# The chunks of the split normalised x laid out with a step of 1040 bytes instead of 1024

## The reference

```python
def _swiglu(h, w_gu, w_down):
    gate, up = jnp.split(h @ w_gu, 2, axis=-1)
    return (jax.nn.silu(gate) * up) @ w_down

x = x + 0.5 * _swiglu(_rmsnorm(x, ffn1_norm), ffn1_w_gu, ffn1_w_down)
x = x + _token_mixing(_rmsnorm(x, mix_norm), w_in, ...)   # merged @ w_out inside
x = x + 0.5 * _swiglu(_rmsnorm(x, ffn2_norm), ffn2_w_gu, ffn2_w_down)
for l in range(2):
    shift, scale, gate = jnp.split(c_act @ w_ada[l] + b_ada[l], 3, axis=-1)
    h = _rmsnorm_2(x, norm_g[l]) * (1.0 + scale) + shift
    z = h @ w_in[l]                                       # 13 pieces of 512
    y = jnp.concatenate([o_fft, o_na, o_ret, o_cv], axis=-1) @ w_out[l]
    x = x + gate * y
```

## Time and profile before

| | |
|---|---|
| median of 3 runs | 3424.93 us (3423.47 to 3428.82) |
| the profiled execution, time | 3430.47 us |
| the profiled execution, span | 3428.7 us |
| mean granted TensorE clock | 0.972 of full speed |
| TensorE matmuls, busy | 3281.0 us (96% of the span) |
| weight loads, busy | 2880.8 us (84%) |
| VectorE, ScalarE, GpSimd, busy | 1777.6, 1456.5, 1780.0 us |
| memory read | 654.15 MB |

### The profile page before, as it was taken

How to read it: one execution, slowest core, us unless ns; L and a number is a source line. 1 busy time by engine, 2 the same in 40 slices (tenths; PEclk the granted TensorE clock), 3 DMA queues, 4 the chain that set the end, 5 groups by cost and what they waited for, 6 DMA issues and landing times.

```text
span 3428.7 us, 47162 instructions
## 1 busy us (share of the span) xinstructions
PE 3281.0 (96%) x19525; PEld 2880.8 (84%) x19525; DVE 1777.6 (52%) x2235; ACT 1456.5 (42%) x1893; POOL 1780.0 (52%) x738
## 2 busy tenths in 40 slices
PE   8999999998999999999999999998998998998988
PEld 6888888888998999887888888887988876998876
DVE  5554554422034478753555554433299654169763
ACT  5444443336554445444444444433333344343343
POOL 4444444437865765674444444444766544666543
PEclk9999999999998999999999999998999998999999
DMA  7887787865764554465888877764544344454444
GB/s 239 260 259 260 257 261 262 268 198 157 173 184 130 153 143 125 127 193 179 262 258 263 261 256 262 267 233 134 154 142 136 117 145 132 143 153 136 123 129 159
DMA packets 479357, 659.36 MB, mean 192 GB/s; under 512 B 63894, under 2 KB 267270, under 8 KB 478886
## 3 DMA queue, kind: packets, MB, share of 16 engines
q1 hardware_dynamic: 478462, 653.64, 60.7%
q0 software_dynamic: 352, 2.46, 0.2%
q10 hardware_dynamic: 328, 0.24, 0.0%
HBM read 654.15 MB, written 2.10 MB: 191 GB/s over the span
## 4 chain that ended last, share of the span: by engine, by line
PE 84%; DVE 11%; ACT 2%; issue 1%; POOL 1%; DMA 0%; ACTq 0%; DVEq 0%
PE ps L758 49%; PE ps L729 26%; DVE U L1834 4%; PE ps L719 2%; PE ps L937 2%; PE ps L954 1%; POOL split_slabs L694 1%; PE ps L1037 1%; DVE U L1718 1%; PE ps L907 1%; PE ps L783 1%; ACT split_slabs L1172 1%; DVE U L1660 0%; PE ps L1093 0%; PE ps L1133 0%
## 5 line engine op out<-in xcount | busy, mean ns | idle before, releaser
L694 POOL TENSOR_TENSOR split_slabs<-stage,split_slabs 128x1024 fp32r<-128x1024 f32 (+1 forms) x730 | 1777.2, 2439 | 1626.6 <-ACT split_slabs L1172 1624.7
L1172 ACT ACTIVATE split_slabs<-stage 128x1024 fp32r<-128x1024 f32 (+1 forms) x1032 | 1086.0, 1056 | 1758.5 <-PE ps L758 954.7
L758 PE MATMUL ps<-split_slabs,h_split 128*128 128x512 f32 x4992 | 1171.5, 396 | 23.2 <-DVE U L1953 12.9
L758 PEld LDWEIGHTS ps<-split_slabs,h_split 128*128 128x128 f32 x4992 | 941.2, 189 | 236.5 <-DVE U L1953 13.7
L729 PE MATMUL ps<-h_split,split_slabs 128*128 128x256 f32 x9072 | 1111.4, 284 | 9.9 <-DVE U L1887 8.0
L729 PEld LDWEIGHTS ps<-h_split,split_slabs 128*128 128x128 f32 x9072 | 1083.6, 193 | 34.3 <-issue 23.0
L1506 DVE TENSOR_TENSOR split_slabs<-stage,split_slabs 128x1024 fp32r<-128x1024 f32 x302 | 379.3, 1256 | 908.5 <-ACT split_slabs L1172 908.5
L758 PE MATMUL ps<-split_slabs,act_split 128*128 128x512 f32 x2112 | 482.1, 390 | 0.0
L758 PEld LDWEIGHTS ps<-split_slabs,act_split 128*128 128x128 f32 x2112 | 395.7, 188 | 82.1
L1834 DVE SCALAR_TENSOR_TENSOR U<-U,params 128x256 f32<-128x256 f32 x240 | 201.5, 910 | 0.0
L1522 DVE SCALAR_TENSOR_TENSOR U<-U,cact 128x512 f32<-128x512 f32 x192 | 189.1, 985 | 6.8
(11 more groups left out here) (196 smaller groups left out, 1650.6 us busy)
## 6 DMA issues: line engine op xcount, KB each, us to landing
stage<-in_w_in SPq DMA_DIRECT2D x360, 512.0 KB, 3.6
stage<-in_ffn_w_gu SPq DMA_DIRECT2D x352, 512.0 KB, 4.5
U<-in_w_ada SPq DMA_DIRECT2D x192, 512.0 KB, 5.8
stage<-in_ffn_w_down SPq DMA_DIRECT2D x176, 512.0 KB, 4.8
stage<-in_w_out SPq DMA_DIRECT2D x96, 512.0 KB, 3.9
stage<-in_w_in SPq DMA_DIRECT2D x80, 128.0 KB, 2.8
stage<-in_w_branch_c SPq DMA_DIRECT2D x32, 192.0 KB, 3.4
stage<-in_cmp_w SPq DMA_DIRECT2D x8, 512.0 KB, 3.8
```

What stands on the lines that cost most here:

```text
L694: nc.gpsimd.tensor_tensor(slab_part(n, 1, size(n)), stage[:, n % RING, 0:size(n)], slab_part(n, 0, size(n)).bitcast(F32), ALU.subtract).th ...
L758: ins = mm(ps[:, 2 * pair + T, :], stationary(kk, tp)[:, T * P:(T + 1) * P], w[wp][:, kk, :], start=first and kk == 0 and i == 0, stop=las ...
L1172: return fn(slab_part(n, 0, size(n)), stage[:, n % RING, 0:size(n)], ACT.Copy)
```

## The change

The step from one chunk of `h_split` to the next becomes 260 elements (1040 bytes) instead of 256 (1024 bytes). Every chunk still has 256 positions; the view `hx` cuts the four added elements off. The tensor grows by 2 x 16 x 16 = 512 bytes in each partition. To make room, `ssq`, `meansq` and `lnms` keep two places instead of six, used in turn (`r % 2`). By the declared sizes that gives 128 + 32 + 32 = 192 bytes back. So `stage` and what follows it up to `ssq` move by 512 bytes, and the arena by 320. Inside the arena nothing moves.

```diff
+HPAD = 4
...
-        hx = sbr("h_split", [P, 2, DC, S])
+        hx = sbr("h_split", [P, 2, DC, S + HPAD])[:, :, :, 0:S]
...
-        ssq = sb("ssq", [P, 6, TT, 4])
-        meansq = sb("meansq", [P, 6, TT])
-        lnms = sb("lnms", [P, 6, TT])
+        ssq = sb("ssq", [P, 2, TT, 4])
+        meansq = sb("meansq", [P, 2, TT])
+        lnms = sb("lnms", [P, 2, TT])
...
-                    fn(ps[:, 5, :], x[:, T, b * WN:(b + 1) * WN], ACT.Square, accum_out=ssq[:, r, T, b:b + 1]
+                    fn(ps[:, 5, :], x[:, T, b * WN:(b + 1) * WN], ACT.Square, accum_out=ssq[:, r % 2, T, b:b + 1]
...
-                chained(fn(lnms[:, r, :], meansq[:, r, :], ACT.Ln, bias=eps, scale=1.0 / D), "ln", r)
-                fn(rstd[:, r, :], lnms[:, r, :], ACT.Exp, scale=-0.5).then_inc(*rstd_ready.mark(r))
+                chained(fn(lnms[:, r % 2, :], meansq[:, r % 2, :], ACT.Ln, bias=eps, scale=1.0 / D), "ln", r)
+                fn(rstd[:, r, :], lnms[:, r % 2, :], ACT.Exp, scale=-0.5).then_inc(*rstd_ready.mark(r))
...
-                v.reduce_sum(meansq[:, r, :], ssq[:, r, :, :], AXX).then_inc(*mean_done.mark(r))
+                v.reduce_sum(meansq[:, r % 2, :], ssq[:, r % 2, :, :], AXX).then_inc(*mean_done.mark(r))
```

## The result

The change makes the kernel slower: 3461.02 us (median of 4 runs) against 3424.34 us, a ratio of 1.0105 with a 95% interval of 1.0087 to 1.0122. The forecast was 3414 us and faster, with a range of 3396 to 3448, and 3461 lies above the range as well. The profiled execution has a span of 3460.6 us, 31.9 us over the one of before.

A forecast was written before the change was run, and what follows sets the result against it. TensorE's matmuls were taken as the bound. Half of a 22.5 us gain, 11.3 us, and zero for all else gave 3413.6 from the median of 3424.9, rounded to 3414 us; range 3396 to 3448.

The forecast's parts named there:

- What bounds the kernel: Whole kernel: TensorE is the bound, its matmuls busy 96% of the span, and slabs from ScalarE come early.
- the prediction's own weights: Shares of matmul time on `h_split` that count on the chain: 0.75 for narrow ones, 0.96 for wide ones.
- The 115.3: Mean ns per narrow matmul with `h_split` before the change, from 14 products at 113.4 or 117.8 ns.
- six slow products: Six of 14 narrow products between 820 and 1000 us, taken at 11.31 us each, 117.8 ns per matmul.
- part 1: Matmuls that read `h_split`: the new step was to make them faster, by 11.3 us.
- full gain: All `h_split` matmuls at the fast rates, 113.4 ns narrow and 227.0 wide: 12.9 + 9.6 = 22.5 us.
- slow rhythm: The slower rate that a narrow product with `h_split` keeps throughout, 117.8 ns a matmul, expected to be left.
- The bound on the loss: Narrow matmuls with `h_split`: all at 120.4 ns, the `heads_split` rate, would cost 34.7 us.
- The further gain: Narrow matmuls with `h_split`: from 113.4 down to about 112 ns, 9.5 us more.
- The slower rival: Chunks off a multiple of 64 bytes slow three narrow matmuls of four to 120.4 ns: 26.0 us, 3451; chance 0.27.
- No effect: Rival: the step changes nothing, rates being set by how a product begins; 3425 us within 7, chance 0.31.
- Parts 2, 3 and 4: Writers of `h_split` (bound 1.0 us), two places for `ssq`, `meansq`, `lnms`, and moved `stage` and arena: zero each.

The follow-up runs named there:

- experiments 3 and 6: Two kernels without the reference's work, each run once: blocks of narrow and wide matmuls with the operands' distance varied; narrow ones at distance 64 ran at 113.3 ns.
- experiment 10: Against the kernel before: wide passes use a view of `h_split` 64 bytes later, split heads moved 192 bytes to distance 64; 3413.63 us, ratio 0.9968.
- experiment 6: Kernel of matmul blocks only, 96 narrow and 48 wide: distance in 16-byte steps, both operands moved, or a matmul put ahead; narrow block at distance 64 11.17 us.
- experiment 1: The changed kernel with its chunks 1024 bytes apart again, all else kept, distance 128 modulo 256; 3471.46 us, ratio 1.0126 against the kernel before.
- experiments 7 to 9: Against the kernel before: two places alone; everything behind `h_split` 256 bytes further; the change without its step, at distance 64. 3427.92, 3425.26, 3428.38 us.

## Why the prediction was wrong, point by point

- *What bounds the kernel* was right: TensorE's rate sets the end, and what its matmuls lose shows in full. By the prediction's own weights, narrow 118.0 - 115.3 = 2.7 ns x 9072 x 0.75 = 18.4 us and wide 2.4 x 4992 x 0.96 = 11.5 us, together 29.9 of the 31.9 us between the two spans. The 115.3 took all six slow products at 11.31 us; with the two of 11.40 and 11.55 us the mean was 115.6, which makes 2.4 ns, 16.3 us and together 27.8.
- *The step that failed* is part 1, "I take half of the full gain", because "a distance that changes after every three matmuls [...] should leave the slow rhythm". The sign was wrong. In place of a gain the rates rose to 118.0 and 231.4 ns. The bound on the loss (34.7 us for all narrow matmuls at 120.4 ns) would have held the narrow part; the wide ones had no loss in it at all. The further gain that was held possible, down to 112 ns, had nothing to it either: no block of experiments 3 and 6 ran under 113.3 ns.
- Behind it was a misreading of the same rows. I saw that the rate goes with the place, took `h_split` for the one that lay badly, and measured its loss against the tensors at distance 0. For the wide matmuls that was right, and experiment 10 collects it. For the narrow ones the rows said the opposite: `heads_split` at distance 0 was the slowest, and `h_split` the only tensor with products at 113.4 ns. For the narrow matmuls `h_split` stood at the best of sixteen distances, so a step that visits all sixteen had nothing to gain there.
- I looked at the distance modulo 1024. The period is 256 bytes, which blocks at known distances showed.
- The mean of the sixteen distances can be checked. At the fifteen from 16 to 240 of experiment 6 the narrow blocks average 11.59 us, against 11.17 at 64. That is 4.4 ns for each matmul over the fast rate and, since 0.43 of the products of before ran 4.4 ns over it already, 2.5 over the kernel before; measured were 2.7 (2.4 with the corrected mean). From start to start, all sixteen distances average 118.1 ns narrow and 232.1 ns wide, against 118.0 and 231.4 in the kernel with the change. The separate values do not come out so: in the four products of that trace whose 96 matmuls are all in the trace and without a pause, the chunk at distance 64 ran at 116.9 ns, not 113.3. So the mean is an estimate that fits; why it fits is not shown.
- *The slower rival* had the right side and about the size (3451 us, narrow at 118.0 of the 120.4 ns it assumed), but the wrong mechanism. Chunks off a multiple of 64 bytes are not it: experiment 1 has all chunks on such multiples and is no faster, and moving both operands by 16 bytes costs nothing. It also left the wide matmuls out. That its size came near is partly luck: all narrow matmuls lost a little, instead of three of four losing 5.1 ns.
- *No effect*: the two rules of the Trainium skill that I set against the forecast fare differently. That TensorE waits for no one (SBUF — State Buffer, section "Who interferes with whom") does not cover what the runs show, 5.75 to 6.02 us for 48 equal matmuls by nothing but the distance of two operands. That a line has 16 bytes (the same page, "Specifications (TRN2)") agrees with experiment 6 as far as one block of each kind tells: for the narrow matmuls 16 bytes of shift are free and 8 are not, 11.17 and 11.85 us.
- *Parts 2, 3 and 4*, costed at zero, were right within the scatter of the runs. The cast kept its time (426 ns, 427 before), and experiments 7 to 9 show nothing for the two places and the shift.
- That two reads of TensorE, the weights and the stream, meet in the same part of a memory with a period of 256 bytes is a reading that fits most of this, but it is argued from rates, and the wide blocks at one distance with two rates (11.27 and 11.15 us) are not explained by it. No run here shows the memory itself. Nor is it settled which starts put a product of the kernel before into the slower rate.

## What to carry to other kernels

This was tried with float32r matmuls of 256 and 512 columns only. When equal matmuls run at different rates in different tensors, work out the distance between their two operands modulo 256 bytes before changing any layout, and try shifts of the whole tensor first: a shift costs a few dozen bytes and keeps one distance for all chunks, while a step padded by 16 bytes spreads them over good and bad ones. Before padding a tensor, ask whether its place is already the good one, and what else the padding moves: here the arena. Narrow and wide passes had different best distances (64 and 0), and two views of one tensor gave both.

## What the runs showed of the hardware that was not expected

- The rate of float32r matmuls depends on the distance between stationary and streamed operand modulo 256 bytes: 256 columns, 113.4 ns at 64 (the faster of two rates), 118.8 (11.40 / 96) at 128 and 119.9 at 0; 512 columns, 226.8 ns at 0, 229.0 at 64 and 232.3 at 128. With 512 columns the place of both operands counts too: moved together by 16 bytes, a block at distance 64 took 11.15 us instead of 11.27.
- At distance 64 a block of narrow matmuls keeps one of two rates to its end, 11.1 or 11.5 us for 96, and 32 more columns ahead of the block switch from one to the other.
- Both operands 8 bytes off a multiple of 16 gave the slowest narrow block of experiment 6 but the first, 11.85 us, and the slowest wide one, 11.77 us.
